# A two-layer hybrid encoder on one core: the first norm's rows spread by transposes, first loads and copies in a new order, head channel factors taken into the output weights

## The chip, the cores and the metric

The kernel runs on one core of one Trainium2 chip. The metric is the device time of one execution in microseconds (us). Before the change three executions took 1148.63, 1150.42 and 1150.18 us; the median is 1150.18 us. The engines are named as in the profile: PE is TensorE's matmul side, PEld its weight loads, DVE VectorE, ACT ScalarE, POOL GpSimd, SP the engine that issues most transfers.

## The reference, cut to what matters

512 tokens of 1024 channels pass an input layer norm and two layers. Everything is in f32.

```
h = layer_norm(x, ln_in_g, ln_in_b)          # (x - mean) * rsqrt(var + eps) * g + b, over 1024 channels
for l in range(2):
    proj = h @ w_in[l]                       # 1024 -> 2048
    ...                                      # four mixers of 256 channels each:
    out_a = windowed attention, 4 heads      # out_b = gated short convolution
    out_c = Fourier mixing                   # out_d = dense attention, 4 heads
    g = grp_g[l]
    mix = concat([rms_norm(o, g[256*i:256*(i+1)]) for i, o in enumerate((out_a, out_b, out_c, out_d))])
    h = layer_norm(DN_ALPHA * h + mix @ w_out[l], ln1_g[l], ln1_b[l])
    ffn = square(relu(h @ w1[l])) @ w2[l]    # 1024 -> 4096 -> 1024
    h = layer_norm(DN_ALPHA * h + ffn, ln2_g[l], ln2_b[l])
return h
```

`rms_norm(o, g)` is `o * rsqrt(mean(o*o) + eps) * g`. The factor `rsqrt(...)` belongs to a token, `g` to a channel; so `g` may be applied to the rows of `w_out` instead of to the columns of `o`.

## The kernel before, in words

**Split products.** A product of f32 operands is made of three: each operand is split into a high part (`_hi`, an fp32r cast, made by ACT) and a low part (`_lo`, what is left, made by DVE or POOL), and `three` (L349 to L351) issues high x high, high x low and low x high. One step of a tile's sum (a `kt`, 128 channels) is three matmuls with 512 columns.

**Weights.** They come in blocks of 128 x 2048 (1 MB). SP loads a block into one of two raw buffers (`w_raw`), ACT casts it to `w_hi`, DVE or POOL subtracts to `w_lo`, PE uses it from a ring of four. SP loads the next block into a raw buffer when `w_lo` of the block in it is made. A block is one instruction on ACT (`split`) and one on DVE or POOL (`split`, `split_low`).

**Tokens.** The 512 tokens are four tiles of 128. For each tile DVE makes the norm: two `row_stats`, `variance`, `centre` (subtract the mean, times the channel factor g: L866, 1024 columns), POOL makes `rstd` with a power, DVE makes `scale` (times rstd, plus the channel offset b: L875, two halves). g and b stand in `rows`, where each of the 128 partitions holds the same 2048 numbers: POOL's queue loads them (1 MB written) before each norm. Then PE turns the tile with eight transposes (L358) into two banks, ACT copies `h_hi` (L640) and DVE makes `h_lo` (L887).

**The start.** SP loads tile 0 and weight block 0, then the rest. PE runs 40 transposes of the identity that nothing reads (`keep_warm`), turns tile 0, runs 24 more, and enters the loop over layers. There the first product (tile 0, eight `kt`) waits for `h_lo` of its half and for `w_lo` of blocks 0 and 1; in the middle of a tile's product the next tile is turned. The low part of block 0 is POOL's, of block 1 DVE's. Tiles are turned into banks 4 and 5, or 6 and 7, in turn.

**Heads.** The 32 attention units run in 33 steps. After four units (a quad q, eight of them) DVE scales the heads by their softmax sums into `head_out` (L1025), ACT sums its squares, POOL multiplies it by the channel factors into `head_gained` (L1243), PE turns that (`turn_quad`, L499), ACT and DVE split it into `mix_hi` and `mix_lo`, and PE multiplies by blocks 10 and 11 of the layer (the rows of `w_out` of the two head groups), in groups of side products that lie between the attention's own steps. DVE adds each of these products into x times the token's factor `group_r`, which POOL makes with a power.

**What sets the order.** Each engine works off its own list as it is written; waits are on semaphores. Nothing is planned by a scheduler.

## Time and profile before

| | |
|---|---|
| median of three executions | 1150.18 us |
| the profiled execution | 1148.63 us, its span 1146.9 us |
| PE busy | 1119.6 us (98%) |
| PE's first product of the network | at 21.9 us |
| DVE, ACT, POOL busy | 611.2, 390.8, 108.9 us |
| HBM read | 102.45 MB, 91 GB/s over the span |

The span is what the profile covers from its first to its last instruction; the execution's own time is 1.7 us longer. PE counts as busy in its 64 transposes of the identity too. Times of instructions are counted from the span's start.

### The profile page before, as it was taken

The page shows a single profiled execution, that of the slowest core. Times are in us where ns is not written, and L with a number is a line of the kernel's source. Part 1 is how long each engine was busy: PE and PEld are TensorE (multiplying, and loading weights), DVE is VectorE, ACT ScalarE, POOL GpSimd, SP SyncE. Part 2 cuts the span into 40 slices and gives each one's busy share as a digit, 9 for nine tenths or more (in the row PEclk, how much of TensorE's full clock was granted, in tenths as well). Part 3 has the DMA queues.
Part 4 walks back from the last instruction along what each step waited for, and adds up shares of the span by engine and source line. Part 5 has one row for each costly group of instructions (what it writes and reads, how often), then busy time and mean ns, then how long its engine had stood idle before and what let it go on. Part 6 is the DMA issues. An engine that isn't in the chain of part 4 may idle for free.

```text
span 1146.9 us, 15152 instructions
## 1 busy us (share of the span) xinstructions
PE 1119.6 (98%) x5528; PEld 936.2 (82%) x5528; DVE 611.2 (53%) x879; ACT 390.8 (34%) x616; POOL 108.9 (9%) x92
## 2 busy tenths in 40 slices
PE   6999999999999999999999999999999999999997
PEld 6888788798888888888888878878888888888886
DVE  6863776765235225226557467677533433433446
ACT  2432665443133124124123246543421421421410
POOL 2200233210000000000012013232000000000002
PEclk9999999999999999999999999999999999999999
DMA  8323112033124113213203320211423123223201
GB/s 311 119 114 119 37 29 101 1 118 147 74 74 147 74 73 140 80 74 124 97 4 147 147 83 20 74 38 45 147 74 147 74 74 136 79 77 122 86 13 74
DMA packets 16675, 106.50 MB, mean 93 GB/s; under 512 B 2000, under 2 KB 2384, under 8 KB 4576
## 3 DMA queue, kind: packets, MB, share of 16 engines
q1 hardware_dynamic: 14976, 98.11, 22.9%
q0 software_dynamic: 1488, 7.43, 2.0%
q8 instruction: 42, 0.69, 0.2%
q14 instruction: 25, 0.20, 0.1%
q10 hardware_dynamic: 144, 0.07, 0.0%
HBM read 102.45 MB, written 2.10 MB: 91 GB/s over the span
## 4 chain that ended last, share of the span: by engine, by line
PE 50%; issue 40%; POOL 4%; DVE 3%; ACT 1%; DMA 1%; DVEq 0%; POOLq 0%; ACTq 0%
PE bank L350 15%; PE bank L349 15%; PE bank L351 15%; POOL w_lo L1209 2%; POOL head_gained L1243 1%; PE bank L441 1%; PE bank L358 1%; POOL rstd L1199 1%; DMA rows<-in_rows 1%; DVE mx L1095 1%; DVE stage L1092 0%; DVE x L866 0%; ACT stage L771 0%; PE bank L379 0%; PE bank L423 0%
## 5 line engine op out<-in xcount | busy, mean ns | idle before, releaser
L349 PE MATMUL bank<-h_hi,w_hi 128*128 128x512 f32 (+1 forms) x704 | 261.0, 371 | 1.6 <-DVE h_lo L887 1.6
L350 PE MATMUL bank<-h_lo,w_hi 128*128 128x512 f32 (+1 forms) x704 | 260.3, 370 | 0.0
L351 PE MATMUL bank<-h_hi,w_lo 128*128 128x512 f32 (+1 forms) x704 | 260.3, 370 | 0.0
L349 PE MATMUL bank<-w_hi,hid_hi 128*128 128x512 f32 x512 | 199.4, 389 | 0.0
L351 PE MATMUL bank<-w_hi,hid_lo 128*128 128x512 f32 x512 | 199.2, 389 | 0.0
L350 PE MATMUL bank<-w_lo,hid_hi 128*128 128x512 f32 x512 | 199.2, 389 | 0.0
L647 ACT CAST w_hi<-w_raw 128x2048 fp32r<-128x2048 f32 x60 | 112.3, 1908 | 243.7 <-PE bank L351 220.3
L349 PEld LDWEIGHTS bank<-h_hi,w_hi 128*128 128x128 f32 x704 | 132.6, 188 | 24.4 <-issue 1.8
L350 PEld LDWEIGHTS bank<-h_lo,w_hi 128*128 128x128 f32 x704 | 132.6, 188 | 22.4
L351 PEld LDWEIGHTS bank<-h_hi,w_lo 128*128 128x128 f32 x704 | 132.6, 188 | 22.4
L1160 DVE TENSOR_TENSOR x<-bank,x 128x512 f32<-128x512 f32 x64 | 44.2, 690 | 195.0 <-PE bank L351 194.5
L846 DVE TENSOR_TENSOR w_lo<-w_raw,w_hi 128x2048 fp32r<-128x2048 f32 x60 | 135.4, 2287 | 21.5 <-ACT w_hi L647 21.5
L1139 DVE TENSOR_TENSOR y<-stage 128x512 f32<-128x512 f32 x64 | 44.2, 691 | 166.4 <-ACT stage L808 165.1
L351 PEld LDWEIGHTS bank<-w_hi,hid_lo 128*128 128x128 f32 x512 | 96.1, 188 | 20.0
L350 PEld LDWEIGHTS bank<-w_lo,hid_hi 128*128 128x128 f32 x512 | 96.1, 188 | 19.9
L349 PEld LDWEIGHTS bank<-w_hi,hid_hi 128*128 128x128 f32 x512 | 96.1, 188 | 19.9
L808 ACT ACTIVATE stage<-bank 128x512 f32<-128x512 f32 x64 | 37.9, 591 | 167.8 <-PE bank L351 167.8
L1199 POOL TENSOR_TENSOR rstd<-var_eps,half_neg 128x1 f32<-128x1 f32 x20 | 22.0, 1098 | 752.2 <-DVE var_eps L860 752.2
L840 DVE TENSOR_TENSOR w_lo<-w_raw,w_hi 128x2048 fp32r<-128x2048 f32 x23 | 52.2, 2289 | 32.2 <-ACT w_hi L634 32.1
L634 ACT CAST w_hi<-w_raw 128x2048 fp32r<-128x2048 f32 x24 | 45.4, 1915 | 62.3 <-PE bank L351 53.6
L1055 DVE SCALAR_TENSOR_TENSOR x<-bank,group_r,x 128x512 f32<-128x512 f32 x64 | 47.8, 750 | 30.9 <-PE bank L351 29.9
L640 ACT CAST h_hi<-bank 128x512 fp32r<-128x512 f32 x34 | 18.5, 590 | 110.1 <-PE bank L358 110.0
(138 smaller groups left out, 1408.5 us busy)
## 6 DMA issues: line engine op xcount, KB each, us to landing
w_raw<-in_weights SPq DMA_DIRECT2D x88, 1024.0 KB, 4.8
rows<-in_rows POOLq DMA_DIRECT2D x5, 1024.0 KB, 4.9
x<-in_x SPq DMA_DIRECT2D x4, 512.0 KB, 9.2
out_h<-x SPq DMA_DIRECT2D x8, 256.0 KB, 2.0
dft<-in_dft SPq DMA_DIRECT2D x1, 1024.0 KB, 13.7
qk_gain<-in_qk_gain POOLq DMA_DIRECT2D x3, 192.0 KB, 3.4
head_gain<-in_head_gain POOLq DMA_DIRECT2D x2, 256.0 KB, 3.6
dq_even<-dq_lo POOLq DMA_DIRECT2D x2, 256.0 KB, 2.9
```

The source lines that it names most:

```text
L349: pe.matmul(dst, s_hi, m_hi, start=first, stop=False)
L350: pe.matmul(dst, s_hi, m_lo, start=False, stop=False)
L351: return pe.matmul(dst, s_lo, m_hi, start=False, stop=last)
L634: act.copy(w_hi[:, b % RING, :], w_raw[:, b % RAW, :]).then_inc(sems["w_hi"], 1)
L647: act.copy(w_hi[:, b % RING, :], w_raw[:, b % RAW, :]).then_inc(sems["w_hi"], 1)
L808: act.activation(stage[:, m % 2, :], bank[m][:], ACT.Relu, scale=ALPHA ** -0.5).then_inc(sems["relu"], 1)
L840: dve.tensor_tensor(w_lo[:, b % RING, :], w_raw[:, b % RAW, :], w_hi[:, b % RING, :].bitcast(F32), ALU.subtract).then_inc(sems["w_lo"], 1)
L846: dve.tensor_tensor(w_lo[:, b % RING, :], w_raw[:, b % RAW, :], w_hi[:, b % RING, :].bitcast(F32), ALU.subtract).then_inc(sems["w_lo"], 1)
L1055: dve.scalar_tensor_tensor(out=xs, in0=b[:], scalar=group_r[:, g, t:t + 1], in1=xs, op0=ALU.mult, op1=ALU.add)\
L1139: dve.tensor_tensor(y[:, m % 2, :], r, r, ALU.mult).then_inc(sems["hidden_square"], 1)
L1160: dve.tensor_tensor(xs, chunk_bank(g, last)[:], xs, ALU.add).then_inc(sems["added"], 1)
L1199: return pool.tensor_tensor(dst, src, half_neg[:, 0:n], ALU.pow)
```

## The change

It has four parts.

**1. The first norm's g and b.** They no longer come as 128 equal rows. `first` is a small load (128 x 16, 8 KB) that holds them with the channel on the partition. PE transposes each of its 16 columns, spread over 128 columns by an access with step 0, and so writes rows of g into banks 2 and 3 and rows of b into banks 6 and 7. `first_norm` reads them there, and centres in two halves of 512. Banks 2 and 3 are then needed for the products of tiles 2 and 3, so PE waits for all four centrings before tile 2.

**2. First loads and copies.** Tile 0 comes in two halves, one on SP's queue and one on ACT's; the identity moves to SP's queue; a weight block of the start comes in two halves. The two blocks at the start of a layer are split in four parts of 512 columns each, and PE waits for a part where it waited for a block. At the start of layer 0 all eight low parts are POOL's. `keep_warm` has 8 and 6 transposes where it had 40 and 24.

**3. Turning.** The next tile is turned one `kt` later, always into banks 4 and 5, and for that waits for `h_lo` of the tile before.

**4. Heads.** POOL's product with the channel factors goes, and the load of the factors. PE turns `head_out` itself. Blocks 10 and 11 take the factors: ACT casts them times a factor per partition, in two halves of 1024 columns, and DVE makes the low part in two halves with one more operand.

```diff
+            sp.dma_start(x[:, 0, 0:BANK], x_in[0, :, 0:BANK]).then_inc(x_half_landed[0], 16)
+            sp.dma_start(ident[:], ident_in).then_inc(ident_landed, 16)
             load_weights(0)
-            sp.wait_ge(x_landed[0], 16)
+            sp.wait_ge(w_half_landed[0], 16)
...
             def turn(l, t):
-                if t >= 2:
-                    wait(pe, l, "h_lo", 2 * (t - 2) + 2)
+                if t >= 1:
+                    wait(pe, l, "h_lo", 2 * (t - 1) + 2)
...
-            keep_warm(40)
+            pe.wait_ge(first_landed, 16)
+            for which in range(2):
+                for half in range(2):
+                    for c in range(4):
+                        k = which * KT + half * 4 + c
+                        last = pe.transpose(first_row(which, half)[:, c * P:(c + 1) * P],
+                                            first[:, k:k + 1].to_broadcast([P, P]), ident[:])
+                    last.then_inc(first_spread, 1)
+            keep_warm(8)
             turn(0, 0)
-            keep_warm(24)
+            keep_warm(6)
...
                     for kt in range(KT):
-                        if kt == KT // 2 and t + 1 < TOK:
+                        if kt == KT // 2 + 1 and t + 1 < TOK:
                             turn(l, t + 1)
                         if kt % 4 == 0:
                             wait(pe, l, "h_lo", 2 * t + kt // 4 + 1)
-                            if t == 0:
-                                block_ready(l, kt // 4)
+                        if t == 0:
+                            part_ready(l, kt // PARTS, kt % PARTS)
+                        if t == 2 and kt == 0:
+                            wait(pe, l, "centred", TOK)
...
-                    wait(pe, l, "out_gained", q + 1)
+                    wait(pe, l, "head_out", q + 1)
...
+            act.dma_start(x[:, 0, BANK:D_MODEL], x_in[0, :, BANK:D_MODEL]).then_inc(x_half_landed[1], 16)
+            act.dma_start(first[:], first_in).then_inc(first_landed, 16)
...
+            def split_gained(l, b, released):
+                act.wait_ge(w_landed[b % RAW], l * (16 * BLOCKS // RAW) + 16 * (b // RAW + 1))
+                wait(act, l, "products", released)
+                for j in range(2):
+                    c, g = slice(j * D_MODEL, (j + 1) * D_MODEL), COL_HEADS + 2 * (b - 10) + j
+                    act.activation(w_hi[:, b % RING, c], w_raw[:, b % RAW, c], ACT.Copy, scale=cols[:, g:g + 1])\
+                       .then_inc(sems["w_hi" if j else "gained_hi"], 1)
...
+            def first_norm(t):
+                halves = [slice(half * BANK, (half + 1) * BANK) for half in range(2)]
+                dve.wait_ge(sems["moments"], t + 1)
+                for half, c in enumerate(halves):
+                    dve.wait_ge(first_spread, half + 1)
+                    dve.scalar_tensor_tensor(out=x[:, t, c], in0=x[:, t, c], scalar=moments[:, t, 0:1], in1=first_row(0, half)[:],
+                                             op0=ALU.subtract, op1=ALU.mult).then_inc(sems["centred"] if half else half_centred, 1)
+                dve.wait_ge(sems["rstd"], t + 1)
+                for half, c in enumerate(halves):
+                    dve.wait_ge(sems["centred"] if half else half_centred, t + 1)
+                    dve.wait_ge(first_spread, 2 + half + 1)
+                    dve.scalar_tensor_tensor(out=x[:, t, c], in0=x[:, t, c], scalar=rstd[:, t:t + 1], in1=first_row(1, half)[:],
+                                             op0=ALU.mult, op1=ALU.add).then_inc(sems["normed"], 1)
...
-            load_rows(0)
             load_params(0)
             pool.wait_ge(const_set, 2)
             layer_norm_rstd(0, 0, 1)
-            split_low(0, 0)
-            layer_norm_rstd(0, 1)
+            for part in range(PARTS):
+                split_low_part(0, 0, part)
+            split_low_part(0, 1, 0)
+            split_low_part(0, 1, 1)
+            layer_norm_rstd(0, 1, 2)
+            split_low_part(0, 1, 2)
+            split_low_part(0, 1, 3)
+            layer_norm_rstd(0, 2)
...
-                    if q >= 2:
-                        wait(pool, l, "mix_turned", q - 1)
-                    pool.tensor_tensor(head_gained[:, q % 2, :], head_out[:, q % 2, :], head_gain[:, g, :], ALU.mult)\
-                        .then_inc(sems["out_gained"], 1)
```

How the instructions stand on three engines, first before and then after.

PE at the start of the program, before; `first` is the small load of g and b, x the tile, and the last row is the first product's first matmul:

```order
L379 MATMUL bank<-ident 128x128 x40
L358 MATMUL bank<-ident,x 128x128 x8
L379 MATMUL bank<-ident 128x128 x24
L384 UNCONDITIONAL_BRANCH
L384 ISA
L286 ISA
L349 MATMUL bank<-w_hi,h_hi 128x512
```

PE at the same place, after:

```order
L407 MATMUL bank<-ident,first 128x128 x16
L400 MATMUL bank<-ident 128x128 x8
L372 MATMUL bank<-ident,x 128x128 x8
L400 MATMUL bank<-ident 128x128 x6
L413 UNCONDITIONAL_BRANCH
L413 ISA
L292 ISA
L363 MATMUL bank<-w_hi,h_hi 128x512
```

Sixteen transposes that write the rows of g and b stand ahead of all else, and the transposes of the identity are 14 where they were 64.

POOL at the start of the program, before; rstd is a tile's factor, w_lo a weight block's low part:

```order
L1196 DMA rows<-in_rows 128x2048
L1189 DMA cols<-in_cols 128x14
L1190 DMA qk_gain<-in_qk_gain 128x384
L1199 ISA
L1199 TENSOR_TENSOR rstd<-var_eps,half_neg 128x1
L1209 TENSOR_TENSOR w_lo<-w_raw,w_hi 128x2048
L1199 TENSOR_TENSOR rstd<-var_eps,half_neg 128x1 x3
```

POOL at the same place, after:

```order
L1288 DMA cols<-in_cols 128x18
L1289 DMA qk_gain<-in_qk_gain 128x384
L1297 ISA
L1297 TENSOR_TENSOR rstd<-var_eps,half_neg 128x1
L1318 TENSOR_TENSOR w_lo<-w_raw,w_hi 128x512 x6
L1297 TENSOR_TENSOR rstd<-var_eps,half_neg 128x1
L1318 TENSOR_TENSOR w_lo<-w_raw,w_hi 128x512 x2
L1297 TENSOR_TENSOR rstd<-var_eps,half_neg 128x1 x2
```

The load of the rows is gone, block 1 has come over from DVE, and the factor of tile 1 stands behind six of the eight parts.

DVE at the start of the program from tile 0's factor to tile 1's low part, before:

```order
L866 SCALAR_TENSOR_TENSOR x<-x,moments,rows 128x1024
L875 SCALAR_TENSOR_TENSOR x<-x,rstd,rows 128x512 x2
L850 BN_STATS bn<-x 128x6 x2
L857 BN_AGGR moments<-bn 128x2
L860 TENSOR_SCALAR var_eps<-moments 128x1
L887 TENSOR_TENSOR h_lo<-bank,h_hi 128x4x128 x2
L866 SCALAR_TENSOR_TENSOR x<-x,moments,rows 128x1024
L875 SCALAR_TENSOR_TENSOR x<-x,rstd,rows 128x512 x2
L840 TENSOR_TENSOR w_lo<-w_raw,w_hi 128x2048
L887 TENSOR_TENSOR h_lo<-bank,h_hi 128x4x128 x2
```

DVE at the same place, after:

```order
L988 SCALAR_TENSOR_TENSOR x<-x,moments,bank 128x512 x2
L994 SCALAR_TENSOR_TENSOR x<-x,rstd,bank 128x512 x2
L969 TENSOR_TENSOR h_lo<-bank,h_hi 128x4x128 x2
L932 BN_STATS bn<-x 128x6 x2
L939 BN_AGGR moments<-bn 128x2
L942 TENSOR_SCALAR var_eps<-moments 128x1
L988 SCALAR_TENSOR_TENSOR x<-x,moments,bank 128x512 x2
L994 SCALAR_TENSOR_TENSOR x<-x,rstd,bank 128x512 x2
L932 BN_STATS bn<-x 128x6 x2
L939 BN_AGGR moments<-bn 128x2
L942 TENSOR_SCALAR var_eps<-moments 128x1
L969 TENSOR_TENSOR h_lo<-bank,h_hi 128x4x128 x2
```

The norms read a bank where they read `rows`, block 1's low part is gone from DVE, and the statistics of tiles 1 and 2 have changed places with low parts.

## Rows read from the trace of the kernel before

**Rows 1.** Who waited for whom on PE, whole span: engine, line, releaser, us, times, longest

```profile
PE bank L358 <- DVE x L875: 5.0, 2, 4.8
...
PE bank L499 <- POOL head_gained L1243: 4.0, 6, 1.3
```

**Rows 2.** Timeline of the start: start us, us, engine, line, operation [idle before, releaser]

```profile
4.67 1.28 DVE L850 BATCH_NORM_STATS2 bn<-x 128x6 f32<-128x512 f32 x2 [3.61 <-DMA x<-in_x]
4.88 7.11 PE L379 MATMUL bank<-ident 128*128 128x128 f32 x40 [4.88 <-DMA ident<-in_ident]
8.30 1.90 ACT L634 CAST w_hi<-w_raw 128x2048 fp32r<-128x2048 f32 x1 [5.49 <-DMA w_raw<-in_weights]
10.28 4.51 POOL L1209 TENSOR_TENSOR w_lo<-w_raw,w_hi 128x2048 fp32r<-128x2048 f32 x1 [3.10 <-ACT w_hi L634]
10.44 5.43 DVE L866 SCALAR_TENSOR_TENSOR x<-x,moments,rows 128x1024 f32<-128x1024 f32 x1 [3.98 <-DMA rows<-in_rows]
16.78 1.87 PE L358 MATMUL bank<-ident,x 128*128 128x128 f32 x8 [4.79 <-DVE x L875]
```

**Rows 3.** Busy time of the engines in stretches: stretch, length, busy (instructions), PE's clock, DMA share, GB/s

```profile
5.00:10.00 5.00, 5.00 (x24) 5.00 (x25) 1.32 (x4) 1.70 (x1) 0.56 (x1) 1.00 0.99 413
...
17.00:18.00 1.00, 1.00 (x6) 0.96 (x5) 1.00 (x3) 0.16 (x1) 0.00 (x0) 0.50 1.08 414
...
20.00:21.00 1.00, 1.00 (x9) 1.00 (x8) 1.00 (x2) 1.00 (x1) 0.00 (x0) 0.83 1.01 386
```

**Rows 4.** The chain that ended last, in order of time, 20 to 36 us: start us, us, what

```profile
24.93 0.45 PE bank L358 x4
25.40 0.60 ACT h_hi L640
...
26.63 0.68 DVE h_lo L887
...
32.78 0.23 PE bank L349
...
35.52 0.23 PE bank L349
```

**Rows 5.** Groups of POOL by form, whole span: busy us, mean ns | idle before us <-releaser

```profile
L1209 POOL TENSOR_TENSOR w_lo<-w_raw,w_hi 128x2048 fp32r<-128x2048 f32 x5 | 22.8, 4565 | 3.1 <-ACT w_hi L634 3.1
L1251 POOL TENSOR_TENSOR dq_lo<-dq,dq_even 128x512 fp32r<-128x512 f32 x4 | 5.2, 1289 | 4.8 <-ACT dq_odd L785 4.8
```

**Rows 6.** Single lines of DVE: duration ns min/median/max, first and last start us, forms

```profile
L1055 DVE SCALAR_TENSOR_TENSOR x<-bank,group_r,x x64: 733/751/753, 127.3 to 790.4; 128x512 f32<-128x512 f32 x64
L866 DVE SCALAR_TENSOR_TENSOR x<-x,moments,rows x20: 1274/1284/5429, 10.4 to 1141.3; 128x1024 f32<-128x1024 f32 x20
```

**Rows 7.** Timeline of the heads, step of quad 6 and of quad 7, layer 0

```profile
212.53 1.69 POOL L1243 TENSOR_TENSOR head_gained<-head_out,head_gain 128x256 f32<-128x256 f32 x1
214.28 0.44 PE L499 MATMUL bank<-ident,head_gained 128*128 128x128 f32 x2 [1.28 <-POOL head_gained L1243]
218.11 0.69 ACT L765 ACTIVATE stage<-bank,neg_mx 128x512 f32<-128x512 f32 x1 [0.97 <-DVE neg_mx L1103]
219.10 0.60 PE L526 MATMUL bank<-ident,stage 128*128 128x128 f32 x4
227.18 0.44 PE L499 MATMUL bank<-ident,head_gained 128*128 128x128 f32 x2 [0.56 <-POOL head_gained L1243]
```

**Rows 8.** Timeline where blocks 11, then 0 and 1 of layer 1, are split

```profile
121.27 0.59 ACT L712 COPY freq<-bank 128x512 f32<-128x512 f32 x1 [2.02 <-PE bank L441]
122.76 1.29 DVE L1068 TENSOR_TENSOR dk_lo<-bank,dk_hi 128x512 fp32r<-128x512 f32 x2 [1.86 <-ACT dk_hi L715]
560.32 4.49 DVE L840 TENSOR_TENSOR w_lo<-w_raw,w_hi 128x2048 fp32r<-128x2048 f32 x2 [1.25 <-ACT w_hi L634]
```

**Rows 9.** DMA issues: what, engine, count, KB each, median us from issue to landing

```profile
head_dft<-in_head_dft SPq DMA_DIRECT2D x1, 128.0 KB, 13.6
cols<-in_cols POOLq DMA_DIRECT2D x3, 7.0 KB, 2.1
```

More of the change, by code:

```diff
@@ L241, in build @@
         cols, _ = place("cols", [P, N_COLS])
+        first, _ = place("first", [P, 2 * KT])
         rope, _ = place("rope", [P, 2, TOK, HEAD_DIM])
@@ L267, in build @@
         x_landed = [sem(f"x_landed{t}") for t in range(TOK)]
+        x_half_landed = [sem(f"x_half_landed{n}") for n in range(2)]
+        w_half_landed = [sem(f"w_half_landed{b}") for b in range(RAW)]
+        first_landed = sem("first_landed")
+        first_spread = sem("first_spread")
+        half_centred = sem("half_centred")
         w_landed = [sem(f"w_landed{s}") for s in range(RAW)]
@@ L288, in turn_bank, with first_row @@
         def turn_bank(which, t, half):
-            return bank[6 + SIDE.index(("t", t, half)) % 2 if which else 4 + 2 * (t % 2) + half]
+            return bank[6 + SIDE.index(("t", t, half)) % 2 if which else 4 + half]
+        def first_row(which, half):
+            return bank[(2, 6)[which] + half]
         def turned_half(which, t, half):
@@ L374, in block_ready, with part_ready @@
                 wait(pe, l, "w_lo", b + 1)
+            def part_ready(l, b, part):
+                if part < PARTS - 1:
+                    wait(pe, l, "w_lo_part", b * (PARTS - 1) + part + 1)
+                else:
+                    block_ready(l, b)
             def keep_warm(n):
@@ L826, in _ @@
                 with act.If(l < DEPTH - 1):
-                    split(l + 1, 0, 12 - CHUNK_G)
-                    split(l + 1, 1, 12 - CHUNK_G)
+                    for b in range(2):
+                        act.wait_ge(w_landed[b], (l + 1) * (16 * BLOCKS // RAW) + 16)
+                        wait(act, l + 1, "products", 12 - CHUNK_G)
+                        for part in range(PARTS):
+                            split_part(l + 1, b, part)
                 stream_high(l + 1, 0, 0, 0)
@@ L841, in split, with split_gained @@
                                   ALU.subtract).then_inc(sems["w_lo"], 1)
+            def split_gained(l, b):
+                for j in range(2):
+                    if j:
+                        wait(dve, l, "w_hi", b + 1)
+                    else:
+                        wait(dve, l, "gained_hi", b - 10 + 1)
+                    c, g = slice(j * D_MODEL, (j + 1) * D_MODEL), COL_HEADS + 2 * (b - 10) + j
+                    dve.scalar_tensor_tensor(out=w_lo[:, b % RING, c], in0=w_raw[:, b % RAW, c], scalar=cols[:, g:g + 1],
+                                             in1=w_hi[:, b % RING, c].bitcast(F32), op0=ALU.mult, op1=ALU.subtract)\
+                       .then_inc(sems["w_lo" if j else "gained_lo"], 1)
             def split_in_chunk(l, c, i):
@@ L1165, in chunk @@
                             with dve.If(l < DEPTH - 1):
-                                split(l + 1, 0)
-                                split(l + 1, 1)
+                                for b in range(2):
+                                    for part in range(PARTS):
+                                        split_part(l + 1, b, part)
                         if last:
@@ L1215, in _ @@
             layer_norm_rstd(0, 0, 1)
-            split_low(0, 0)
-            layer_norm_rstd(0, 1)
+            for part in range(PARTS):
+                split_low_part(0, 0, part)
[5 more added lines that the diff above has]
+            layer_norm_rstd(0, 2)
             with pool.Fori(0, DEPTH) as l:
@@ L1230, in _ @@
                     power(group_r[:, g, :], mean_sq[:, g, :], TOK).then_inc(sems["group_rstd"], 1)
-                wait(pool, l, "head_gain", 16)
                 for q in range(8):
```

116 lines of the change are left out of this document (72 added, 44 removed).

## The prediction, made before the changed kernel ran

> **What bounds the kernel now.** I read the page first: PE is busy for 1119.6 of 1146.9 us, so a gain can come only out of PE's idle time and out of what PE does for nothing. The list of waits on PE then says where it idles: longest before the turning of tile 0, 4.8 us, and in the heads, 4.0 us in six waits for POOL's `head_gained` [rows 1]. The timeline of the start shows the rest. PE gets the identity at 4.88 us, runs 40 transposes that nobody reads, idles 4.79 us, turns tile 0 at 16.78 us and has its first useful product at 21.9 us. What holds tile 0 back is visible on DVE: its statistics are made from 4.67 us on, but `centre` waits 3.98 us for the load of `rows`, starts at 10.44 us, and then takes 5.43 us [rows 2], where the same instruction takes 1.28 us as a rule [rows 6]. Beside it POOL makes block 0's low part, from 10.28 to 14.79 us [rows 2]. After that PE is nearly gapless, and a shift of its work in the first 35 us moves the end by as much. As the reference point I take the first matmul of tile 2's product, at 35.52 us [rows 4].
>
> **Part 1 and 2, the start.** The sum follows PE, POOL and DVE as the orders stand.
>
> *The rows of g and b.* PE waits for the identity and for `first`. The identity came at 4.88 us [rows 2] and keeps its place behind as few bytes. `first` is 8 KB behind a quarter megabyte on ACT's queue, issued near 1.7 us. No row shows it. From below: 7 KB took 2.1 us, but the identity holds PE to 4.9 us anyway. From above: 128 KB at the end of the long queue took 13.6 us [rows 9], which gives 15.3 us. I take 5.0 us, since tile 0's half megabyte, ahead of everything, was there at 4.67 us [rows 2]. At the engine's start 24 transposes took 5.00 us [rows 3], 0.21 us each. The 16 new ones and the 8 of `keep_warm` are also 24: PE is free to turn tile 0 at 10.0 us.
>
> *Tile 0's norm* hides in that. Statistics from about 4.5 us, mean and variance by 6.1 us, centring in two halves, scaling once b's first row is there (12 transposes, 7.5 us), done near 9.1 us. A half that reads a bank I price at 0.75 us, as the 64 `x<-bank,group_r,x` of the same form, which never took more than 0.753 us [rows 6]; the 1.28 us of `centre` with 1024 columns would make it 0.64 us. The stall of 5.43 us has no successor here: those 64 ran beside POOL's later low parts too, and none was stretched. So DVE's 6 us and the wait for `rows` go; what is late next is PE's own list of transposes, by about 0.9 us.
>
> *Turning tile 0.* From the first transpose to both high halves takes 1.70 us, to both low halves 2.38 us (24.93 to 26.63 and 27.31) [rows 4]: 11.7 and 12.4 us. Block 0's parts 0 and 1 are made by then: the block landed at 8.30 us behind other loads [rows 2], and its first half has fewer ahead.
>
> *The weights are what is late next.* ACT makes part 2 of block 0 only after the high halves: a quarter of 1.90 us [rows 2], 12.2 us. Then POOL works through four parts without a gap, parts 2 and 3 of block 0, parts 0 and 1 of block 1. A part of 512 columns lies between a quarter of 4.565 us, 1.14 us, and the 1.29 us of `dq_lo` in the same form [rows 5]. I take 1.2 us: 17.0 us. Behind them on POOL's list stands tile 1's rstd, 0.56 us [rows 3]: 17.6 us. DVE has long centred tile 1 and scales its halves in 0.75 us each, 18.3 and 19.1 us; the second half's four transposes end near 19.5 us. PE meanwhile has run `kt` 0 to 4 as the parts came, and has idled about half of the time; behind its waiting turn of tile 1 stand `kt` 5 to 7, whose last part is ready at 20.0 us. A `kt` takes 0.685 us (four from 32.78 to 35.52) [rows 4]: tile 0 is done at 21.5 us.
>
> *Tile 1 and the new wait.* Five `kt`, 3.4 us, bring PE to the turning of tile 2 at 24.9 us; eight transposes (0.9 us) and three `kt` bring it to 27.8 us. Then it waits for the fourth centring, which stands on DVE behind tile 2's low halves: 24.9 + 2.4 + 2 x 0.75 = 28.8 us. This wait of 1.0 us is new, and all of PE is queued behind it. Tile 2 starts at 28.8 us instead of 35.5: **6.7 us** saved. From there on the pace is as before. Turning one `kt` later leaves 0.9 + 2.05 = 2.95 us for the 2.4 us that the low halves need, so it costs nothing; a DVE late by over 0.5 us would show.
>
> Later loads don't matter: block 2 is loaded when block 0's low part is made, at about 14.6 us where it was 14.8, and needed 18 us later by my times.
>
> **Part 3, the halves and parts elsewhere.** Blocks 10 and 11 cost ACT and DVE one more instruction each and a scale, some 0.3 us. Behind block 11, the tighter one, ACT has 2.02 us idle before its second `freq` copy and DVE 1.86 us before `dk_lo` [rows 8]. Both hide it; with that cover gone it would be 0.3 us a layer. At the start of layer 1 eight parts cost DVE about 0.4 us more than two blocks, but it waited 1.25 us for ACT's first whole block [rows 8] and now waits for a part: minus 0.8 to plus 0.4 us on DVE, and PE had no wait here. I set nothing.
>
> **Part 4, the heads.** In each layer PE waits 1.28, 0.56 and 0.16 us for `head_gained`, 4.0 us in both [rows 1, 7]. POOL needs 1.69 us there, beside DVE's `centre` [rows 7]. With `head_out` turned directly all three are gone. But the 1.28 us of quad 6 are not all kept: two steps later the transposes start at 219.10 us, and the exponential whose result they turn ends at 218.80 us [rows 7], bound to DVE's maximum and not to PE. So only 0.3 us can be kept there. The 0.56 us of quad 7 stand behind the last attention step and are kept. 0.86 us a layer, **1.7 us**; the ends are 1.1 us (quad 7 alone) and 4.0 us.
>
> **The sum.** 6.7 + 1.7 = 8.4 us off the profiled execution's 1148.63 us gives 1140.2 us. That execution is the fastest of three, 1.55 us below their median; I put half of that on top: **1141.0 us**.
>
> **Rivals.**
>
> *A: the clock falls in the gaps.* Before, PE idled 4.79 us, and its clock then stood at 0.50 of 2.4 GHz, that is 1.2 GHz, in 17 to 18 us, and came back within 20 to 21 us [rows 3]. After the change PE has half-idle 7 us from 12 to 18 us, with its longest gap under 2 us. For the rival: 14 transposes keep it warm and not 64. Against: no gap is near 4.79 us. If it falls, the work from 18.3 us on starts at 1.2 GHz, for the 3.4 us that it took before (16.8 to some 20.2 us), which loses half of them: 1.7 us, and 1142.7 us. [...]
>
> *B: the heads give all they waited.* If the exponential also comes earlier, since POOL no longer contends with DVE, the heads save 4.0 us: 1137.9 + 0.8 = 1138.7 us. For it: POOL's 1.69 us fall away. Against: `centre` beside them took its usual time, since its largest value but for the start's is near 1.28 us.
>
> *C: POOL's parts are held up, and the start gains nothing.* Ten DVE instructions of 0.75 us lie beside POOL's parts. Were each to stop POOL, four parts and rstd end 5 to 7 us later: the start saves 0 to 2 us, 1146 to 1149 us. Against: POOL's five whole low parts average 4.565 us and differ little although DVE worked beside them [rows 5].
>
> *D, slower: `first` lands late.* PE can issue nothing before it. It decides from the point where 8.4 us are used up, a landing at 13.4 us. At 15.3 us, as 13.6 us after issue [rows 9], the kernel takes 1.9 us more than before, 1150.5 us. Against: that row is a load behind some 5 MB in one queue, this one behind 0.25 MB. The Trainium skill says in "DMA: Bandwidth & Descriptors", section "Queues, rings and completion order", that a DMA engine takes packets from its queues in turn; by that the weights on SP's queue would not hold it up, and no row before shows such a load.
>
> **Chances.** Forecast 0.62, A 0.17, B 0.12, C 0.05, D 0.02, and 0.02 for a slower outcome that I have not named. The forecast's own spread is 1139 to 1143 us: the pace of a part (0.2 to 0.4 us over four), the landing of `first` (up to 1 us) and the median's offset. A range for 8 in 10 reaches down past B, whose heads could meet a start that is 1 us better, to 1137.5 us, and up past A joined with a late `first` and heads of 1.1 us, to 1145.5 us. Within 0.2% (2.3 us, about what a measurement of this kernel tells from no change) lie C and half of D: 0.06. Faster 0.91, slower 0.03.
>
> **What would show it.** In the changed profile: the turn of tile 0 near 10.0 us; the first matmul near 12 us; POOL's parts of 1.2 us in a gapless row of four; the turn of tile 1 waiting until 18.3 us; tile 2 at 28.8 us after a wait of 1.0 us for DVE; no wait of the heads' turns, and new ones of PE for ACT's exponential. Wrong it would be if DVE's halves took more than 0.8 us, if PE's clock stood at 0.50 behind 18 us, or if PE waited for weights in tile 1.

## The result and the profile after

| | before | changed |
|---|---|---|
| median of 5 runs, us | 1150.16 (1148.63 to 1150.42) | 1143.91 (1143.07 to 1144.24) |
| ratio, 95% interval | | 0.9949 (0.9934 to 0.9963) |
| profiled execution, us | 1148.63 | 1143.91 |
| its span, us | 1146.9 | 1142.2 |
| PE busy, us | 1119.6 | 1118.0 |

The kernel is faster by 0.5%. The forecast was 1141.0 us in 1137.5 to 1145.5. The two profiled executions differ by 4.7 us, where the forecast's sum was 8.4 us.

Waits on PE, answering to [rows 1]: releaser, then us in total, times, longest.

```profile
PE bank L407 <- DMA first<-in_first: 4.9, 1, 4.9
PE bank L557 <- ACT stage L828: 2.4, 7, 0.6
PE bank L363 <- DVE h_lo L969: 2.3, 5, 0.8
PE bank L363 <- POOL w_lo L1318: 2.0, 2, 1.8
PE bank L575 <- ACT pT L813: 2.0, 4, 0.7
PE bank L372 <- DVE x L994: 1.6, 1, 1.6
PE bank L363 <- DVE x L988: 0.8, 1, 0.8
```

Both rows of before are gone: 5.0 us for the norm of tiles 0 and 1, 4.0 us for `head_gained`. What took their place at the start is POOL's low parts, the scaling of tile 1 (L994) and the centring (L988).

The start as a timeline, answering to [rows 2] (start us, us, engine, line, operation, idle before and its releaser):

```profile
4.92 3.65 PE L407 MATMUL bank<-ident,first 128*128 128x128 f32 x16 [4.92 <-DMA first<-in_first]
6.12 1.53 DVE L988 SCALAR_TENSOR_TENSOR x<-x,moments,bank 128x512 f32<-128x512 f32 x2
8.36 1.53 PE L400 MATMUL bank<-ident 128*128 128x128 f32 x8
8.85 0.33 SPq L329 DMA_DIRECT2D x<-in_x  x1
9.22 0.43 SPq L324 DMA_DIRECT2D w_raw<-in_weights  x1
9.55 5.03 POOL L1318 TENSOR_TENSOR w_lo<-w_raw,w_hi 128x512 fp32r<-128x512 f32 x4 [2.81 <-ACT w_hi L664]
9.73 1.04 PE L372 MATMUL bank<-ident,x 128*128 128x128 f32 x8
11.84 0.49 PE L363 MATMUL bank<-w_hi,h_hi 128*128 128x512 f32 x1 [0.41 <-DVE h_lo L969]
15.35 1.14 ACT L664 CAST w_hi<-w_raw 128x512 fp32r<-128x512 f32 x2 [2.86 <-DMA w_raw<-in_weights]
16.04 2.51 POOL L1318 TENSOR_TENSOR w_lo<-w_raw,w_hi 128x512 fp32r<-128x512 f32 x2 [1.47 <-ACT w_hi L664]
17.36 0.50 PE L363 MATMUL bank<-w_hi,h_hi 128*128 128x512 f32 x1 [1.77 <-POOL w_lo L1318]
18.52 0.55 POOL L1297 TENSOR_TENSOR rstd<-var_eps,half_neg 128x1 f32<-128x1 f32 x1
19.10 1.40 DVE L994 SCALAR_TENSOR_TENSOR x<-x,rstd,bank 128x512 f32<-128x512 f32 x2 [3.79 <-POOL rstd L1297]
19.91 1.97 PE L372 MATMUL bank<-ident,x 128*128 128x128 f32 x8 [1.58 <-DVE x L994]
31.68 0.50 PE L363 MATMUL bank<-w_hi,h_hi 128*128 128x512 f32 x1 [0.82 <-DVE x L988]
```

Up to 11.84 us all is as forecast. Then SP's rows tell what is new: tile 1 and block 1 are asked for only at 8.85 and 9.22 us, since SP waits for block 0's first half (this wait is called the hold below). Block 1 lands at 15.35 us, ACT and POOL stand idle for it, PE has two gaps of 1.77 and 1.58 us, and its turn of tile 1 takes 1.97 us where tile 0's took 1.04 us. The windows say why (stretch, length, busy time with count of PE, PEld, DVE, ACT, POOL, then granted clock, DMA share, GB/s), answering to [rows 3]:

```profile
4.00:5.00 1.00, 0.07 (x1) 0.10 (x2) 0.78 (x2) 0.00 (x0) 0.00 (x0) 1.00 0.66 183
5.00:6.00 1.00, 1.00 (x5) 1.00 (x6) 0.86 (x3) 0.00 (x0) 0.00 (x0) 1.00 0.87 175
8.00:9.00 1.00, 1.00 (x6) 1.00 (x5) 0.92 (x2) 0.14 (x1) 0.00 (x0) 1.00 0.40 164
9.00:10.00 1.00, 1.00 (x9) 1.00 (x9) 0.42 (x1) 0.99 (x2) 0.45 (x1) 1.00 0.37 102
...
20.00:21.00 1.00, 1.00 (x5) 1.00 (x6) 1.00 (x2) 0.00 (x0) 1.00 (x2) 0.50 0.96 398
21.00:22.00 1.00, 1.00 (x6) 1.00 (x5) 0.90 (x3) 0.68 (x2) 0.54 (x1) 0.50 1.07 420
22.00:23.00 1.00, 1.00 (x4) 0.71 (x4) 0.96 (x4) 0.49 (x1) 0.55 (x1) 0.50 1.04 419
...
692.00:694.00 2.00, 1.88 (x6) 1.69 (x7) 1.20 (x3) 1.46 (x6) 0.29 (x1) 0.51 0.00 0
694.00:696.00 2.00, 2.00 (x10) 1.51 (x10) 0.38 (x1) 1.52 (x5) 0.00 (x0) 0.64 0.04 8
```

The clock stands at 0.50 (1.2 GHz) for three microseconds behind the two gaps, and falls once more in the heads of layer 1. The loads run at 102 to 183 GB/s in the four stretches shown between 4 and 10 us (325 and 316 GB/s in the two between them), where in the kernel before 5 to 10 us had 413 GB/s.

Heads of layer 0, answering to [rows 7]: the exponential and the transposes that wait for it, and the turn of quad 7.

```profile
214.42 0.69 ACT L822 ACTIVATE stage<-bank,neg_mx 128x512 f32<-128x512 f32 x1 [1.53 <-DVE neg_mx L1201]
215.25 0.66 PE L557 MATMUL bank<-ident,stage 128*128 128x128 f32 x4
222.70 0.38 PE L530 MATMUL bank<-ident,head_out 128*128 128x128 f32 x2
```

The offset between the traces grows along the program: 3.57 us where tile 2 is under way; 3.70 us behind quad 5 (211.01 less 207.31); 3.85 us at the transposes behind quad 6 (219.10 less 215.25); 4.54 us once quad 7 is turned; 4.84 us ahead of layer 1's heads; 3.69 us where the clock has fallen and come back in them; 4.63 us behind them; 4.7 us at the end.

### The profile page after: what moved, and what is told of

It reads as the page before. It is cut to its first block, busy times and chain, and to the rows that moved or that the text cites. A ratio compares the mean times of both kernels' runs of the same rounds, so it can differ in the third digit from the quotient of the medians.

```text
span 1142.2 us, 15092 instructions
## 1 busy us (share of the span) xinstructions
PE 1118.0 (98%) x5494; PEld 933.6 (82%) x5494; DVE 606.8 (53%) x892; ACT 393.1 (34%) x632; POOL 94.4 (8%) x80
## 4 chain that ended last, share of the span: by engine, by line
PE 59%; issue 32%; DVE 4%; ACT 1%; POOL 1%; DVEq 0%; POOLq 0%; ACTq 0%
PE bank L363 17%; PE bank L364 17%; PE bank L365 17%; PE bank L575 2%; PE bank L557 2%; PE bank L472 1%; PE bank L548 1%; PE bank L549 1%; ACT stage L828 1%; PE bank L372 1%; POOL rstd L1297 1%; DVE mx L1193 1%; DVE stage L1190 1%; DVE x L948 0%; DVE mx L1199 0%
## 5 line engine op out<-in xcount | busy, mean ns | idle before, releaser
L694 ACT CAST w_hi<-w_raw 128x2048 fp32r<-128x2048 f32 x60 | 112.3, 1908 | 244.8 <-PE bank L365 220.3
L917 DVE TENSOR_TENSOR w_lo<-w_raw,w_hi 128x2048 fp32r<-128x2048 f32 x60 | 135.4, 2287 | 21.5 <-ACT w_hi L694 21.5
L363 PE MATMUL bank<-w_hi,mix_hi 128*128 128x512 f32 x128 | 55.7, 435 | 0.5 <-DVE h_lo L969 0.4
L363 PE MATMUL bank<-w_hi,h_hi 128*128 128x512 f32 x128 | 51.2, 400 | 3.3 <-POOL w_lo L1318 2.0
```

Source lines behind the costliest of these rows:

```text
L363: pe.matmul(dst, s_hi, m_hi, start=first, stop=False)
L694: act.copy(w_hi[:, b % RING, :], w_raw[:, b % RAW, :]).then_inc(sems["w_hi"], 1)
L917: dve.tensor_tensor(w_lo[:, b % RING, :], w_raw[:, b % RAW, :], w_hi[:, b % RING, :].bitcast(F32), ALU.subtract).then_inc(sems["w_lo"], 1)
```

## The experiments

Before's median on the chips of these runs was 1150.0 to 1150.4 us. All are edits of the changed kernel, unless the text says otherwise; "tile 2" is the start of its first product, 31.68 us in the changed kernel, read in one trace each. A trace's start is uncertain by some 1 us for a reason that is in no edit (the last section), so "tile 2" is read together with the time at which tile 0 is turned, 9.73 us in the changed kernel.

| run | median, us | range | tile 2, us |
|---|---|---|---|
| changed kernel | 1143.91 | 1143.07 to 1144.24 | 31.68 |
| no hold | 1141.76 | 1141.56 to 1142.18 | 29.67 |
| whole blocks | 1143.93 | 1142.93 to 1144.74 | 32.48 |
| filled gaps | 1142.59 | 1141.12 to 1142.98 | 30.09 |
| no hold, filled gaps | 1141.57 | 1140.90 to 1142.00 | 29.15 |
| and rstd first | 1140.88 | 1140.09 to 1141.60 | 28.51 |
| and centring first | 1140.01 | 1138.94 to 1140.36 | 26.78 |
| loads as before | 1144.38 | 1143.35 to 1145.08 | 32.59 |
| parameters late | 1142.73 | 1142.13 to 1143.23 | 30.30 |
| all moves | 1138.99 | 1138.22 to 1139.37 | 27.21 |
| all moves, `first` padded | 1139.10 | 1138.41 to 1139.48 | 27.29 |
| before, heads alone | 1147.52 | 1146.53 to 1147.86 | |
| before, parameters first | 1150.29 | one run | |

**No hold.**

```
-            sp.wait_ge(w_half_landed[0], 16)
             load_tile(1)
```

> The changed kernel without SP's wait for the first half of block 0, so that tile 1, block 1 and the rest are issued at once. Theory L (loads): in the changed kernel block 1's first half landed only at 15.35 us, since SP held everything behind block 0's first half until 8.85 us and the DMA share fell to 0.4 in 8 to 10 us; POOL then stood 1.47 us and PE 1.77 us. Without the hold block 1's first half should land by 13 us, POOL's parts run without a gap, tile 2 start at about 30.4 us instead of 31.95, and the time fall by 1.5 us (by 2.5 us if the clock then stays up). Rival H (short rows): the loads are slow because a half block has rows of 4 KB and not 8 KB; then the landing moves by under 1 us and the time by under 0.7 us.

1141.76 us, ratio to before 0.9930 (0.9917 to 0.9944). Block 1 and PE's turn of tile 1:

```profile
12.94 2.42 ACT L663 CAST w_hi<-w_raw 128x512 fp32r<-128x512 f32 x4 [1.24 <-DMA w_raw<-in_weights]
17.64 1.77 PE L371 MATMUL bank<-ident,x 128*128 128x128 f32 x8 [1.57 <-DVE x L993]
```

Block 1 was there 2.4 us sooner, tile 2 began 2.0 us sooner, and the time fell by 2.15 us. So the hold was the price of the late block. How large a price is less sure: tile 0 was turned at 8.96 us in this trace, 0.8 us sooner than in the changed kernel's, and POOL's second chain of parts hangs on that (11.26 us), so some 1.2 of the 2.0 us are the edit's in this pair, where the medians say 2.15 us. The clock fell here too (0.50 from 18.0 to 21.4 us). The turn still waited 1.57 us, now for tile 1's rstd, which stood in POOL's queue until 16.23 us behind two parts of block 1, though its variance had been there since 13.44 us.

**Whole blocks**, to see whether short rows make the load slow.

```
-                c = slice(0, BLOCK // 2)
-                sp.dma_start(w_raw[:, b, c], w_in[b, :, c]).then_inc(w_half_landed[b], 16)
-                c = slice(BLOCK // 2, BLOCK)
-                sp.dma_start(w_raw[:, b, c], w_in[b, :, c]).then_inc(w_landed[b], 16)
+                sp.dma_start(w_raw[:, b, :], w_in[b]).then_inc(w_landed[b], 16)
...
-            sp.wait_ge(w_half_landed[0], 16)
+            sp.wait_ge(x_half_landed[0], 16)
...
```

> The changed kernel with blocks 0 and 1 loaded whole, as before the change (rows of 8 KB), and SP's hold only for tile 0's first half. The copies stay in parts. Both theories expect a gain; L as in the run without the hold (block 1 there by 13 us, 1.5 us less time), H more: block 0 whole by 8.3 us as in the kernel before, 0.5 us earlier than the first half alone landed now, block 1 by 11.5 us, the time 2 to 2.5 us less. If it is slower than the changed kernel, halves were worth their cost.

1143.93 us. Block 0, whole, was there only at 11.03 us, where before it came at 8.30 us [rows 2]:

```profile
11.03 1.14 ACT L661 CAST w_hi<-w_raw 128x512 fp32r<-128x512 f32 x2 [7.72 <-DMA w_raw<-in_weights]
```

The length of the rows is not the cause. Neither theory's gain came: the time is that of the changed kernel. With SP waiting only for tile 0's first half, POOL's eight parts ran without a gap, but from 11.72 us and not from 9.55 us; what the shorter wait gave, the late start of block 0 took.

**Heads alone**: the kernel before, with only the channel factors taken into blocks 10 and 11 and `head_out` turned directly.

```
-                    wait(pe, l, "out_gained", q + 1)
+                    wait(pe, l, "head_out", q + 1)
...
-                split(l, 10, 14)
-                split(l, 11, 16)
+                split_gained(l, 10, 14)
+                split_gained(l, 11, 16)
```

> The kernel before with part 4 alone: head_out turned directly, POOL's product and its load gone, blocks 10 and 11 scaled. By the prediction 1.7 us less than before (0.86 us a layer); by the positions in the changed kernel's trace 0.95 us in layer 0 (from 3.58 to 4.53 us ahead) and as much in layer 1 if PE's clock does not fall there: 1.9 us. Rival: the whole 4.0 us. If the fall of the clock at 692 us in the changed kernel's layer 1 belongs to the shorter waits of the heads, it shows here too, and takes 0.95 us back.

1147.52 us, ratio 0.9979 (0.9969 to 0.9988): 2.5 us off the median of before, with 1.4 to 3.6 us in the interval. The forecast's 1.7 us lies in it. Laid beside the trace of before, PE gained 1.0 us in the heads of layer 0 and 0.95 us in those of layer 1, and lost 1.1 us where its clock fell to 0.50 near 697 us; so the two profiled executions (1147.52 and 1148.63 us) differ by only 1.1 us.

**Filled gaps**: 12 transposes of the identity ahead of each of slices 4 and 5 of tile 0 (a slice is a `kt`, counted from 0), in layer 0 only.

```
+                        if t == 0 and kt in (KT // 2, KT // 2 + 1):
+                            with pe.If(l < 1):
+                                for _ in range(12):
+                                    pe.transpose(bank[1][:, 0:P], ident[:], ident[:])
```

> The changed kernel with 12 more transposes of the identity, in layer 0 only, ahead of the fifth and ahead of the sixth kt of tile 0, where PE idled 1.77 and 1.58 us. Theory C (clock): the fall to 0.50 at 19.8 us comes from these gaps; filled, the turning of tile 1 takes 1.04 us and not 1.97, the three matmuls behind it 0.69 us and not 1.4, and tile 2 starts 1.2 to 1.7 us earlier, the time falls by as much. Rival: the chain is bound by POOL and DVE there, so that the time moves by under 0.5 us; or the branch costs what the clock gives.

1142.59 us. No window of the start shows a fall:

```profile
20.00:21.00 1.00, 1.00 (x8) 0.77 (x7) 1.00 (x3) 0.71 (x2) 1.00 (x1) 1.00 1.06 442
21.00:22.00 1.00, 1.00 (x6) 0.82 (x5) 0.86 (x4) 0.47 (x1) 0.26 (x2) 1.00 1.02 396
```

The turn of tile 1 and the next two slices took 3.78 us in the changed kernel (19.91 to 23.69) and 2.55 us here (19.53 to 22.08): 1.2 us is what the low clock cost. The median fell by 1.3 us. The two traces differ by more, 2.8 us, as the clock did not fall in this one's heads either. The Trainium skill tells in "TensorE: Matmul & The Clock Gate", section "HAM oscillation — how this bites in real kernels", of a kernel whose clock falls again in each wait for data between its groups of matmuls, waits longer than those here; in this case gaps of 1.77 and 1.58 us were enough.

**No hold, filled gaps**: both edits.

> The changed kernel without the hold ahead of tile 1's load, and with 12 transposes of the identity ahead of slices 4 and 5 of tile 0 in layer 0: the two experiments that gained on their own (1141.76 and 1142.59 against 1143.91 us), put together. If what they gain has two separate causes (tile 1 and block 1 landing late; the clock falling in the gaps of tile 0), the gains add: tile 2 begins near 28.6 us (29.94 with the hold gone alone, less the 1.3 to 1.6 us that the low clock cost there), and the time is near 1140.4 us (1139.9 to 1141.2). If both act by one wait, it stays near the better of the two, 1141.3 to 1142.

1141.57 us, less than 0.2 us below no hold alone, with overlapping ranges: the medians did not add. Some of the reason is in the traces. PE's turn of tile 0 was at 9.85 us here and at 8.96 us in the trace of no hold (the last section says why), so 0.9 us of tile 2's start is not the edit's. Why the medians lie only 0.2 us apart is not shown beyond that. The profiled start, 29.15 us, is 0.35 us from the forecast's 28.8 us.

**Rstd first**: no hold, POOL takes tile 1's rstd ahead of block 1, and the filling transposes are 6 ahead of slice 4 and 3 ahead of each of slices 6 and 7, where they were 12 and 12 ahead of slices 4 and 5. The cut shows POOL's part.

```
...
+            layer_norm_rstd(0, 1, 2)
             split_low_part(0, 1, 0)
             split_low_part(0, 1, 1)
-            layer_norm_rstd(0, 1, 2)
```

> The same, and GpSimd takes tile 1's reciprocal deviation ahead of block 1's four parts instead of between its second and third; the filling transposes are 6 ahead of slice 4 and 3 ahead of slices 6 and 7. With the hold gone, that power waited in GpSimd's queue until 16.23 us though its variance stood from 13.44, and TensorE's turn of tile 1 waited for it until 17.64. If GpSimd's queue sets the end of tile 0 from there (theory), the power now runs at 13.8, the turn of tile 1 at about 16.3 with no wait, block 1's four parts end at 19.4 instead of 19.3, tile 0 ends at 20.1, tile 1 at 26.6, and tile 2 begins behind the wait for the centred tile 3 at about 27.8: 1139.6 us (1138.8 to 1140.4). If the turn of tile 1 is not what sets it (rival: landing of tile 1 or block 1's high parts), tile 2 begins no earlier than in the run before this one, and the time is within 0.4 us of it.

1140.88 us: 0.7 us less, and tile 2 0.64 us sooner, for both edits together. PE's turn of tile 1 came at 17.44 us with no wait, and POOL's last part ended at 20.3 us, so the end of tile 0 is set by the parts and no longer by the turn. The step is as expected (0.8 us), the level is 1.3 us higher: the second chain of POOL's parts started at 12.27 us and not at 11.26 us as in the trace of no hold, from which the expectation was worked out.

**Centring first**: the kernel of the run before, and DVE centres tile 3 ahead of tile 2's low halves.

```
             input_stats(3)
+            first_centre(3)
             stream_low(0, 0, 2)
-            first_norm(3)
+            first_scale(3)
```

> The kernel with no hold, filled gaps and tile 1's power ahead of block 1, and on VectorE the centring of tile 3 ahead of tile 2's low halves. Tile 2's products wait in TensorE's queue for the last read of the banks that hold the row (0.82 us in the changed kernel; more if tile 1 ends sooner, about 1.2 us here, from 26.6 to 27.8). If that wait is the last cost of the rows in banks, it goes, tile 2 begins at 26.7 to 27, and the time is 1.0 us less than with the power moved alone: 1138.6 us (1138 to 1139.5). If the low halves of tile 2 are then late instead (rival: they come 1.4 us later), the same 1 us is lost at their wait and the time stays within 0.3 us of it.

1140.01 us, 0.9 us less. Tile 2 began 1.7 us sooner, 0.7 us of it because tile 0 was turned at 9.24 us and not at 9.96 us. DVE's two rows, and no wait of PE behind them:

```profile
23.50 1.41 DVE L991 SCALAR_TENSOR_TENSOR x<-x,moments,bank 128x512 f32<-128x512 f32 x2
25.11 1.29 DVE L972 TENSOR_TENSOR h_lo<-bank,h_hi 128x512 fp32r<-128x512 f32 x2 [0.20 <-ACT h_hi L690]
```

The wait of 0.8 us for the last reader of the row's banks was real, and the order alone takes it away.

**Loads as before**: tile 0 whole on SP, `first` and then the identity on ACT's queue.

```
-            sp.dma_start(x[:, 0, 0:BANK], x_in[0, :, 0:BANK]).then_inc(x_half_landed[0], 16)
-            sp.dma_start(ident[:], ident_in).then_inc(ident_landed, 16)
+            load_tile(0)
             load_weights(0)
-            sp.wait_ge(w_half_landed[0], 16)
+            sp.wait_ge(x_landed[0], 16)
...
```

> The changed kernel with tile 0 loaded whole on SyncE's queue and the identity on ScalarE's, as before, `first` ahead of it there; tile 1 held until tile 0 has landed; blocks 0 and 1 still in two halves. In the changed kernel's trace the load rate in 4 to 6 us is 183 and 175 GB/s where it was 426 and 401, and block 0's first half lands at 8.86 us, the whole block at about 11.3, against 8.30 for the whole block before. If the split of tile 0 over two queues, with the identity ahead of the weights, costs this rate, block 0's first half lands by 6.5 and the block by 8.5, tile 1 by 11, and the time is 1141.5 to 1142.5 us. If the small packets of `first` cost it (rival), or the missing requests behind block 0, the first half lands at 7.3 to 8.9 and the time is 1141.5 us or more by the hold alone: then the landing of block 0's first half and the rate in 4 to 6 us tell it, not the time.

1144.38 us. The rate in 4 to 6 us stayed at 236 and 221 GB/s, so the split of tile 0 does not cause the dip. Block 0's first half came at 6.93 us, between what the theory and its rival expected (by 6.5 us; 7.3 to 8.9 us). As a test of the time it was spoilt: behind `first` the identity came at 7.1 us, and the turn of tile 0 at 11.75 us, 2 us late. That the time was still only 0.5 us above the changed kernel's fits the cost of the hold, which here was for tile 0 alone, but does not isolate it.

**Parameters late**: the request for `cols` and `qk_gain` behind tile 2's rstd.

```
-            load_params(0)
             pool.wait_ge(const_set, 2)
...
-            layer_norm_rstd(0, 2)
+            layer_norm_rstd(0, 2, 3)
+            load_params(0)
+            layer_norm_rstd(0, 3)
```

> The changed kernel, with layer 0's parameters (`cols` and the broadcast `qk_gain`, 201 KB in 256 packets of 1.5 KB or less) asked for on GpSimd's queue behind tile 2's reciprocal deviation, near 22 us, instead of at 1.4 us. Before the change 1 MB of rows stood ahead of them in that queue, `qk_gain` landed 12.8 us into the span, and the dip of the load rate (249 and 193 GB/s) was at 10 to 12 us; in the changed kernel it lands at 8.5 us and the dip is at 4 to 6 us (183 and 175 GB/s). If these small packets take block 0's share of the DMA engines (theory), the rate in 4 to 6 us is above 300 GB/s, block 0's first half lands at 6.3 to 7.5 us instead of 8.86, the hold ends with it, block 1's first half lands by 13.5 instead of 15.35, and the time is 1141.5 to 1142.8 us. If it is only that too little is asked for behind block 0 (rival: the hold alone), the first half still lands at 8.3 to 8.9 and the time stays at 1143.5 to 1144.3 us.

The time, 1142.73 us, fell as the theory wanted, but its mechanism did not show:

```profile
4.00:5.00 1.00, 0.11 (x1) 0.14 (x2) 0.77 (x2) 0.00 (x0) 0.00 (x0) 1.00 0.74 110
5.00:6.00 1.00, 1.00 (x6) 1.00 (x7) 0.86 (x3) 0.00 (x0) 0.00 (x0) 1.00 0.92 139
```

The rate was lower still, and block 0's first half came at 8.30 us. Block 1's first half came at 14.11 us instead of 15.35 us, which is the size of the gain; why, is not shown.

**The kernel before with its parameters ahead of the rows.**

```
-            load_rows(0)
             load_params(0)
+            load_rows(0)
```

> The kernel before with the two requests for the parameters ahead of the one for the rows on GpSimd's queue; nothing else. If the parameters' small packets cost the engines their rate, the dip moves from 10 to 12 us to 4 to 8 us (below 300 GB/s where it was over 400), block 0 lands 1 to 2.5 us later than at 8.30, and the rows later too. If they cost nothing (rival: it is the changed kernel's other loads), the rate in 4 to 8 us stays at 390 GB/s or more and block 0 lands at 8.3 to 8.8. The time isn't what tells; one run.

One run, 1150.29 us. The dip moved with the packets, but block 0 landed at 8.09 us, not later than at 8.30 us:

```profile
4.00:5.00 1.00, 0.10 (x1) 0.10 (x2) 0.34 (x1) 0.00 (x0) 0.00 (x0) 1.00 1.09 445
...
7.00:8.00 1.00, 1.00 (x8) 1.00 (x7) 0.00 (x0) 0.00 (x0) 0.17 (x1) 1.00 0.75 68
```

So in this run these packets made a dip and did not delay the weights.

**All moves**: no hold, centring first, parameters late, block 1's first part ahead of tile 1's rstd, and 8 filling transposes ahead of tile 1's turn alone.

> All that gained, and the parameters late: no hold, tile 3 centred ahead of tile 2's low halves, parameters behind tile 2's power; on GpSimd block 1's first part ahead of tile 1's power; 8 filling transposes ahead of tile 1's turn alone. If block 0 lands by 8.3 us, GpSimd's parts of block 0 end near 12.5 instead of 14.05, block 1's last part near 18.0 to 18.5 instead of 19.55, tile 1's turn is then bound by VectorE (scale of tile 1 from 14.9) and ends at 17.3, tile 0 ends near 19.3 instead of 20.3, tile 2 begins near 25.9 instead of 26.9, and the time is 1139.0 us (1138.2 to 1139.8) against 1140.0. If the load is no longer what GpSimd waits for (rival), it is within 0.4 us of 1140.0.

1138.99 us, ratio 0.9905 (0.9890 to 0.9920): the lowest median, 4.9 us below the changed kernel. The time is as expected, its place isn't. Block 0's first half landed at 8.79 us, tile 1 was turned at 17.49 us, and tile 2 began at 27.21 us, not at 25.9. PE's clock did not fall in the heads of this trace, while in that of centring first it stood at 0.87 and 0.79 in 680 to 692 us. Laid side by side, centring first was 0.4 us ahead until there, and 0.7 us behind from there on. So of the 1.0 us between these two medians, none is shown to come from the start.

**`first` padded** to 512 bytes a partition, the rest as in all moves.

```
-        first, _ = place("first", [P, 2 * KT])
+        first, _ = place("first", [P, P], at=at_hid)
...
```

> The kernel with all moves, and `first` padded from 16 to 128 numbers a partition: its 128 packets carry 512 bytes instead of 64, in a stretch of SBUF that is free until the attention. The parameters being late did not lift the load rate in 4 to 6 us (110 and 139 GB/s with them late and the hold, 177 and 254 with all moves; 426 and 401 in the kernel before), so of the small packets only those of `first` are left as a cause. If they hold up the engines (theory), the rate in 4 to 6 us rises above 330 GB/s, block 0's first half lands by 7 us instead of 8.79, and the time is 0 to 0.8 us below the 1138.99 us of all moves. If it is not the size of these packets (rival: the million bytes of the one broadcast row were what kept the rate high before, and weights and tokens alone come no faster at the start), the rate stays at 110 to 300 GB/s, `first` lands 0.1 us later, and the time is within 0.4 us of 1139.0.

1139.10 us, and the rival was right:

```profile
4.00:5.00 1.00, 0.09 (x1) 0.12 (x2) 0.78 (x2) 0.00 (x0) 0.00 (x0) 1.00 0.85 155
5.00:6.00 1.00, 1.00 (x5) 1.00 (x6) 0.86 (x3) 0.00 (x0) 0.00 (x0) 1.00 0.88 123
```

Neither the halves, nor the split of tile 0, nor the parameters, nor the packet size of `first` alone makes the slow load at 4 to 6 us. These are single traces that scatter: in the four with no hold and the same first loads the rate in 4 to 5 us was 195 to 305 GB/s, and block 0's first half landed at 7.01 to 8.13 us. What was not tried is the request for a million bytes of one broadcast row, which in the kernel before stood beside these loads. No run put that back, so this stays open.

## Why the prediction was right or wrong

**Right, to 0.3 us: the way to the first product.** `first` at 4.92 us (forecast 5.0), tile 0 turned at 9.73 (10.0), first product at 11.84 (12). A half that reads a bank took 0.70 to 0.78 us (0.75), a part on POOL 1.26 us (1.2). The stall of 5.43 us has no successor.

**Wrong: "POOL works through four parts without a gap".** POOL worked off block 0, and then waited 1.47 us for block 1, so tile 1's rstd started at 18.52 us and not at 17.0. The forecast priced what the change loads first, and had no term for what SP's new hold makes late. Its sentence "later loads don't matter" looked at block 2, and passed over block 1 and tile 1. With the hold taken away, the median fell by 2.15 us.

**Rival A happened**, at 0.17 of the chances, and beside the forecast's own path. Its price was put at 1.7 us; measured are 1.2 us in the trace and 1.3 us in the median. That the longest gap would be under 2 us was right; that this would keep the clock was not.

**The start, added up.** Forecast: tile 2 at 28.8 us. Turn of tile 1 1.6 us late (19.91 against 18.3), 1.2 us of low clock, and 0.1 us besides, make 31.7 us: it is 31.68. The wait for the centring was 0.82 us (1.0). The saving reads 3.57 us and not 6.7 us; of the 3.1 us between, 0.2 to 0.3 us come from the reference point, since the chain's row at 35.52 us stands 0.16 us behind the first product's start, and that product is 0.11 us longer in the changed kernel.

**Right: the heads, 1.9 us where 1.7 us were forecast.** The waits for `head_gained` are gone. Quad 6 kept only 0.15 us of its 1.28 us (forecast 0.3), as the exponential still waits for DVE's maximum; quad 5 kept 0.13 of its 0.16 us, which the forecast left out; quad 7 kept 0.69 us (0.56). Together 0.97 us in layer 0 against 0.86 us. In layer 1 the waits gave 0.94 us more (from 3.69 to 4.63 us), but before that the clock stood at 0.51 and 0.64 in 692 to 696 us and took 1.15 us. So the heads gave 1.9 us in this pair of traces, and 1.95 us in that of heads alone; rival B's 4.0 us did not come. The 2.5 us in the medians of heads alone is no cleaner price, as most of before's executions hold a lower clock than its profiled one (below); the executions of both with a mean clock of 0.997 lie 1.8 to 2.2 us apart.

**Part 3** was put at nothing. Between the heads of the two layers the offset grew by 0.3 us. It grew by 0.1 us there in the trace of heads alone, which has neither part 3 nor the four parts of a block; the other 0.2 us no run isolates.

**The whole sum.** 8.4 us were forecast and the traces differ by 4.7 us. Of the 3.7 us between, the start took 3.1 us and the fall of the clock in layer 1's heads 1.15 us, for which the forecast had no term; the heads gave 0.2 us and the start of layer 1 0.3 us more than forecast.

**The median's offset.** Half of 1.55 us was added. The changed kernel's profiled run is its median, so nothing was due: the sum's 1140.2 us missed by 3.7 us, the forecast of 1141.0 us by 2.9 us. The gain in medians is 6.25 us, the gain in traces 4.7 us, because before's profile was its fastest run; the last section shows where 1.65 us go in a run of nearly the same kernel. Among the rivals, C's 1149 us does not follow from its own terms (a start that saves 0 to 2 us and the heads' 1.7 us give 1145.7 to 1147.7 us with the offset), and D's 1150.5 us leaves the offset out; neither happened.

**With its two conditions met.** With the hold gone and the gaps filled, which the forecast took for granted, the kernel takes 1141.57 us (forecast 1141.0 us), and tile 2 starts at 29.15 us (28.8 us).

## What to carry to other kernels

When a change makes a queue wait, list every request behind that wait with the time it is needed, not only the load that the wait protects: here a hold meant to let one half-block through first cost 2.15 us in the medians, and the half-block came no sooner for it: at 8.30 to 8.96 us in three traces with this hold, at 7.01 to 8.89 us in six without. When waits of PE become several short ones in place of one long one, look at the granted clock behind them before counting the idle time as saved; a dozen useless transposes in a gap that is there anyway are the cheap test. And a buffer that is freed by the last reader of four is freed by an order: moving that reader ahead of work that was not yet needed gained 0.9 us here.

## What the runs showed of the hardware that was not expected

**The first transposes change pace at a time of their own.** From 4.9 us on one takes about 0.22 us, and at some point 0.11 us, with a granted clock of 1.00 in the windows throughout. The point lay at about 7.8 us in the run without the hold, at about 9.4 us in the changed kernel and at 10.3 us in whole blocks (the 8 transposes of `keep_warm` took 1.04 us without the hold and 1.53 us in the changed kernel):

```profile
8.08 1.04 PE L399 MATMUL bank<-ident 128*128 128x128 f32 x8
```

It moved the turn of tile 0 between 8.96 and 10.11 us in runs with the same instructions ahead of it (8.96 us both in no hold and, with the hold, in parameters late), so a single trace of the start is uncertain by some 1 us.

**The clock falls in the heads without a long gap.** PE's longest idle time ahead of the fall at 692 us was 0.61 us:

```profile
692.12 0.90 PE L557 MATMUL bank<-ident,stage 128*128 128x128 f32 x3 [0.61 <-ACT stage L828]
```

It does not need the shorter waits of the new heads: the kernel before with its parameters first has the old heads, and its clock fell at the same instruction. The instruction, and the window of 698 to 700 us with a granted clock of 0.50:

```profile
697.52 0.90 PE L526 MATMUL bank<-ident,stage 128*128 128x128 f32 x3 [0.64 <-ACT stage L771]
698.00:700.00 2.00, 2.00 (x7) 1.61 (x7) 0.61 (x2) 1.54 (x5) 0.39 (x1) 0.50 0.03 8
```

That fall cost 1.0 us, a longer low clock at the start most of the rest, and that run ended 1.65 us behind the profiled run of before, which has no fall in the heads. The clock also fell in layer 1's heads in heads alone, no hold, whole blocks, centring first and loads as before, and near 131 to 138 us, in layer 0's heads, in no hold with filled gaps, rstd first, parameters late and `first` padded; it fell in neither place in filled gaps and all moves. Run by run the time goes with the mean granted clock: of before's runs those at 0.997 took 1148.35 to 1148.75 us, those at 0.994 took 1150.0 to 1151.2 us. Two profiles can so differ by 1 to 2 us without any edit.
